# Encoder layer with expert-choice MoE on one core: splits, row loads, routing rounds, waves and norm sums in a new order, and idle turns at the head

## The reference

```python
h = rmsnorm(x, norm_mix)
u_b, u_c, u_x, u_f = split(h @ w_in)                  # 1024 -> 3*512 + 512
y_conv = rmsnorm(short_conv_mixer(u_b, u_c, u_x, conv_w), g_conv)
y_four = rmsnorm(real(fft2(u_f, axes=(seq, group of 64))), g_fourier)
x = x + concat(y_conv, y_four) @ w_out
h = rmsnorm(x, norm_ffn)
aff = softmax(h @ w_router)                           # 16 experts
gates, idx = top_k(aff.T, cap)                        # cap = 2*t//16 rows each
ye = (silu(xe @ w_gate) * (xe @ w_up)) @ w_down       # xe = h[idx], d_ff = 2816
x = x + scatter_add(ye * gates)
y = rmsnorm(x, norm_final)
```

## Time and profile before

| | |
|---|---|
| median of 3 runs | 2486.88 us (2484.79 to 2487.03) |
| the profiled execution | 2488.08 us, span 2486.2 us |
| mean granted clock of TensorE | 0.989 |
| PE busy | 2424.6 us (98%) |
| VectorE busy | 1611.8 us (65%) |
| ScalarE busy | 1358.4 us (55%) |
| GpSimd busy | 261.6 us (11%) |
| DMA | 628.13 MB, 253 GB/s |

### The profile page before, as it was taken

How to read it: one execution, slowest core, us unless ns; L and a number is a source line. 1 busy time by engine, 2 the same in 40 slices (tenths; PEclk the granted TensorE clock), 3 DMA queues, 4 the chain that set the end, 5 groups by cost and what they waited for, 6 DMA issues and landing times.

```text
span 2486.2 us, 45242 instructions
## 1 busy us (share of the span) xinstructions
PE 2424.6 (98%) x18368; PEld 1901.5 (76%) x18368; DVE 1611.8 (65%) x1331; ACT 1358.4 (55%) x1258; POOL 261.6 (11%) x234
## 2 busy tenths in 40 slices
PE   8999998699999999999999999999999999999996
PEld 7988887577777777777777777777777777777775
DVE  5443438766666666667666666666767676767665
ACT  6322343355555556565656565655555555555564
POOL 0020143102010202010201020102010101010102
PEclk9999999799999999999999999999999999999998
DMA  6002242568787878787878787878787878787877
GB/s 208 22 26 71 85 160 102 180 257 317 261 316 263 317 262 319 262 317 262 318 262 318 262 318 261 319 257 320 260 320 261 319 261 318 260 319 261 318 287 279
DMA packets 295966, 628.13 MB, mean 253 GB/s; under 512 B 21360, under 2 KB 72688, under 8 KB 295536
## 3 DMA queue, kind: packets, MB, share of 16 engines
q1 hardware_dynamic: 284160, 587.87, 64.2%
q0 software_dynamic: 11632, 37.51, 5.0%
HBM read 599.10 MB, written 26.21 MB: 252 GB/s over the span
## 4 chain that ended last, share of the span: by engine, by line
PE 92%; DVE 3%; issue 2%; DMA 1%; ACT 1%; POOL 0%; SPq 0%; POOLq 0%; DVEq 0%; ACTq 0%
PE ps L386 21%; PE ps L387 20%; PE ps L388 20%; PE ps L1618 12%; PE ps L1370 8%; PE ps L1626 6%; PE ps L1636 2%; DVE i L1135 1%; PE ps L1575 1%; DVE v L1133 1%; DVE A L1138 0%; PE ps L1390 0%; PE ps L1645 0%; DMA fx<-acc_dram 0%; DMA raw<-in_w_gate_dram 0%
## 5 line engine op out<-in xcount | busy, mean ns | idle before, releaser
L1249 DVE TENSOR_TENSOR spl_l<-raw,spl_h 128x2048 fp32r<-128x2048 f32 x528 | 1209.1, 2292 | 542.3 <-ACT spl_h L842 537.5
L842 ACT ACTIVATE spl_h<-raw 128x2048 fp32r<-128x2048 f32 x528 | 1011.8, 1917 | 583.6 <-PE ps L388 393.1
L386 PE MATMUL ps<-spl_h,xT 128*128 128x512 f32 x1408 | 554.1, 394 | 0.5 <-DVE xT L1254 0.4
L387 PE MATMUL ps<-spl_l,xT 128*128 128x512 f32 x1408 | 549.0, 390 | 0.0
L388 PE MATMUL ps<-spl_h,xT 128*128 128x512 f32 x1408 | 548.2, 389 | 0.0
L386 PEld LDWEIGHTS ps<-spl_h,xT 128*128 128x128 f32 x1408 | 264.2, 188 | 75.6 <-issue 19.1
L1618 PE MATMUL ps<-raw,xTs 128*32 128x256 f32 (+1 forms) x6144 | 314.2, 362 | 0.0
L388 PEld LDWEIGHTS ps<-spl_h,xT 128*128 128x128 f32 x1408 | 264.3, 188 | 56.1
L387 PEld LDWEIGHTS ps<-spl_l,xT 128*128 128x128 f32 x1408 | 264.3, 188 | 53.0
L386 PE MATMUL ps<-spl_h,g 128*128 128x512 f32 x704 | 279.1, 397 | 3.3 <-DVE spl_l L1249 3.3
L387 PE MATMUL ps<-spl_l,g 128*128 128x512 f32 x704 | 275.4, 391 | 0.0
(11 more groups left out here) (247 smaller groups left out, 1999.1 us busy)
## 6 DMA issues: line engine op xcount, KB each, us to landing
raw<-in_w_up_dram SPq DMA_DIRECT2D x352, 512.0 KB, 7.9
raw<-in_w_gate_dram SPq DMA_DIRECT2D x352, 512.0 KB, 9.3
raw<-in_w_down_dram SPq DMA_DIRECT2D x176, 1024.0 KB, 14.7
win_raw<-in_w_in_dram SPq DMA_DIRECT2D x16, 512.0 KB, 3.9
xt<-in_x_dram SPq DMA_DIRECT2D x10, 512.0 KB, 9.7
xr<-in_x_dram SPq DMA_DIRECT2D x10, 512.0 KB, 4.1
acc_dram<-xr SPq DMA_DIRECT2D x10, 512.0 KB, 2.7
xn_dram<-xn SPq DMA_DIRECT2D x10, 512.0 KB, 2.9
```

What stands on the lines that cost most here:

```text
L386: eng.matmul(o, a_h, b_h, start=first, stop=False, skip_group_check=True)
L387: eng.matmul(o, a_h, b_l, start=False, stop=False, skip_group_check=True)
L842: act.activation(spl_h[:, i % SPL, :], raw[:, slot_of(i), :], ACT.Copy).then_inc(sh_ok, 1)
L1249: dve.tensor_tensor(spl_l[:, i % SPL, :], raw[:, slot_of(i), :], spl_h[:, i % SPL, :].bitcast(F32), ALU.subtract).then_inc(sl_ok, 1)
```

## The change

It has seven parts. (1) At the head PE runs 24 transposes of the identity ahead of its first turns and 7 behind the first two. (2) In round 6 the waves stand behind steps 0, 2 and 4 instead of 0, 1 and 2. (3) The ten norm sums of tile 0 are split in 2, 4 and 4 and stand inside `half(..., 1, ...)`, and with them the wait for the last split of w_out (wol_ok) stands ahead of all of them. (4) In tiles 1, 2, 3, 5, 6, 7 and 9 the turn of the rows stands ahead of step 3 of the second half instead of ahead of the half. (5) VectorE's rounds 4 to 15 of half 0 move: rows 5 and 7 have one round less, none stands between the early rounds and the second sum, and three instead of one stand behind row 7. (6) Around the first gather the idle turns are 50 and 14 instead of 40 and 10. (7) In the last expert rows 3 to 5 move from unit INS+6 to behind the splits of unit INS+7's turn, and POOL issues the loads of rows 6 to 9 ahead of the stores of rows 3 to 5; FX is 7.

```diff
-FX = 6
-ROWS_STOP = {2: (0, 1, 2), 3: (3, 4, 5)}
-ROWS_UNIT = {INS + 8: (6, 7), INS + 9: (8, 9)}
+FX = 7
+ROWS_STOP = {2: (0, 1, 2)}
+ROWS_UNIT = {INS + 7: (3, 4, 5), INS + 8: (6, 7), INS + 9: (8, 9)}
...
-            for t in range(3, FX):
+            for t in range(3, FX - 1):
                 load_rows(t)
             for t in range(3):
                 store_rows(t)
...
-            for t in range(3, FX):
-                store_rows(t)
             pool.wait_ge(pe_s, (E - 1) * SAMPLE + NC + 1)
-            for t in range(FX, TILES):
+            for t in range(FX - 1, TILES):
                 load_rows(t)
-            for t in range(FX, TILES):
+            for t in range(3, TILES):
                 store_rows(t)
...
             rows(4, 0, None, None, None, None, (0, 0, 1))
-            rows(5, 1, (0, 1, 3), None, None, (0, 4, 1), (0, 5, 1))
-            rows(6, 0, (0, 6, 2), None, None, (0, 8, 1), (0, 9, 1))
-            rows(7, 1, (0, 10, 3), None, None, (0, 13, 1), (0, 14, 1))
-            top(0, 15, 1)
+            rows(5, 1, (0, 1, 3), None, None, None, (0, 4, 1))
+            rows(6, 0, (0, 5, 3), None, None, None, (0, 8, 1))
+            rows(7, 1, (0, 9, 3), None, None, None, (0, 12, 1))
+            top(0, 13, 3)
...
             pe.wait_ge(ident_ok, 4)
+            idle_turns(24)
             for t in range(2):
                 turn_x(t)
+            idle_turns(7)
...
-                    if 3 <= n < 3 + JH and k < 3:
-                        waves(n - 3, k)
+                    at = (0, 2, 4) if n == 2 + JH else (0, 1, 2)
+                    if 3 <= n < 3 + JH and k in at:
+                        waves(n - 3, at.index(k))
...
+                ends = [n for n in range(2) if t == GROUPS[n][1]]
                 if t == 0:
                     pe.wait_ge(qs_ok, JH - 1)
                     pe.wait_ge(rn_rt, 1)
-                    norm_sums(qc, 0)
                     pe.wait_ge(wol_ok, KD)
+                    between = {0: lambda: norm_sums(qc, 0, 0, 2), 1: lambda: norm_sums(qc, 0, 2, 6),
+                               2: lambda: norm_sums(qc, 0, 6, TILES)}
+                elif ends:
+                    rows_turned(t - 1)
+                    between = {1: lambda: router(ends[0]), 2: lambda: logits_turned(ends[0])}
                 else:
-                    rows_turned(t - 1)
+                    between = {3: lambda: rows_turned(t - 1)}
                 pe.wait_ge(ysl_ok, t * 2 + 2)
                 pe.wait_ge(x2_ok, t + 1)
-                ends = [n for n in range(2) if t == GROUPS[n][1]]
-                half(t, s, 1, of_done, {1: lambda: router(ends[0]), 2: lambda: logits_turned(ends[0])} if ends else {})
+                half(t, s, 1, of_done, between)
...
-            idle_turns(40)
+            idle_turns(50)
             gathered(1)
-            idle_turns(10)
+            idle_turns(14)
```

More of the change, by code:

```diff
@@ L1437, in waves, with norm_sums, idle_turns @@
                 last.then_inc(ds_done, 1)
-            def norm_sums(q, col):
-                for t in range(TILES):
+            def norm_sums(q, col, a=0, b=TILES):
+                for t in range(a, b):
                     last = pe.matmul(bank(7)[:, col + t:col + t + 1], q[:, t * P:(t + 1) * P], ones[:, 0:1],
                                      start=True, stop=True)
-                last.then_inc(nrm_ps, 1)
+                if b == TILES:
+                    last.then_inc(nrm_ps, 1)
+            def idle_turns(count):
+                for _ in range(count):
+                    pe.transpose(bank(0)[:, 0:P], ident[:, :], ident[:, :])
             pe.wait_ge(ident_ok, 4)
+            idle_turns(24)
             for t in range(2):
                 turn_x(t)
+            idle_turns(7)
             project_ahead(0, 0, 256, 2, {(0, 7): 2, (1, 7): 3})
@@ L1526, in rows @@
                     pe.wait_ge(rn_rt, 1)
-                    norm_sums(qc, 0)
                     pe.wait_ge(wol_ok, KD)
+                    between = {0: lambda: norm_sums(qc, 0, 0, 2), 1: lambda: norm_sums(qc, 0, 2, 6),
[3 more added lines that the diff above has]
+                    between = {1: lambda: router(ends[0]), 2: lambda: logits_turned(ends[0])}
                 else:
-                    rows_turned(t - 1)
+                    between = {3: lambda: rows_turned(t - 1)}
                 pe.wait_ge(ysl_ok, t * 2 + 2)
                 pe.wait_ge(x2_ok, t + 1)
-                ends = [n for n in range(2) if t == GROUPS[n][1]]
-                half(t, s, 1, of_done, {1: lambda: router(ends[0]), 2: lambda: logits_turned(ends[0])} if ends else {})
+                half(t, s, 1, of_done, between)
                 for n in ends:
                     group_turned(n)
-            def idle_turns(count):
-                for _ in range(count):
-                    pe.transpose(bank(0)[:, 0:P], ident[:, :], ident[:, :])
             def group_turned(n):
```

## The result

The changed kernel takes 2567.28 us (median of 4 runs, 2565.16 to 2570.07), beside 2486.84 of the kernel before on the same chip: ratio 1.0326, 95% interval 1.0308 to 1.0344. It is 80 us slower, where I had forecast 10 us faster.

A forecast was written before the change was run, and what follows sets the result against it. PE was taken to bound the kernel, with 92% of the chain. Terms -1.8 - 2.4 + 2.7 - 3.4 + 0.2 - 6.2 = -10.9 took 2488.08 to 2477.2 us; range 2475 to 2479.3, with rivals 1 to 3 2474.2 to 2480.5.

The forecast's parts named there:

- the one that ended slower (5): Output projection, tile 0: idling before the norm sums drops PE's clock and the sums keep it low; 2506 us, chance 0.01.
- Head, -1.8: Kernel start: 24 and 7 idle turns delay nothing and raise PE's clock for later work; -1.8 us, bounds 0 and -2.
- Rival 1: Head without gain: PE's clock is low again when tile 2 comes, since two waits stay; 2479.0 us, chance 0.15.
- Waves, -2.4: Last Fourier block: the new order removes PE's 0.92 us wait and the 1.5 us clock fall behind it; -2.4 us.
- Norm sums, +2.7: Output projection, tile 0: split sums stand on the path, tile 1 late; even chance of a clock fall; +2.7 us.
- Rounds, -3.4: Routing on VectorE: moved rounds and row turns remove PE's waits of 1.80 and 1.58 us; -3.4 us.
- Gather, +0.2: First gather: 50 and 14 idle turns end slightly later than the gathered rows need; +0.2 us, bounds 0 and +0.8.
- The end, -6.2: Last expert: earlier last split and loads of rows 6 to 9 bring the last scaling forward; -6.2 us, bounds -3.5 and -7.

The follow-up runs named there:

- no_turns: The changed kernel with its 45 added idle turns (24 and 7 at the head, 10 and 4 at the gather) taken out again; 2483.1 us, ratio 0.9975.
- tail_alone: The kernel before with only the change's part at the end (last expert's norms, last split, loads ahead of stores); 2479.9 us, ratio 0.9969.
- slot_128: The whole changed kernel with PE's expert loop made to begin at slot 128 of a 256-instruction fetch block; 2483.0 us, ratio 0.9976.
- slot_32: The whole changed kernel with PE's expert loop made to begin at slot 32 of a fetch block; 2555.6 us, ratio 1.0270.
- slot_192: The whole changed kernel with PE's expert loop made to begin at slot 192 of a fetch block; 2488.7 us, ratio 1.0002.
- sums_alone: The kernel before with only the norm sums dealt out over the second half, and the moved wait for wol_ok; 2495.6 us, ratio 1.0029.
- sums_back_128: The changed kernel with PE's loop at slot 128 and the norm sums in one piece ahead of the second half; 2476.9 us, ratio 0.9958.
- slot_64: The whole changed kernel with PE's expert loop made to begin at slot 64 of a fetch block; 2546.2 us, ratio 1.0235.
- shift_44: The kernel before with 88 waits (44 instructions, no matmuls) added on PE at the head; 2507.6 us, ratio 1.0080.
- sums_back_173: The changed kernel with the norm sums in one piece and PE's loop at slot 173; 2477.6 us, ratio 0.9962.

## Why the prediction was wrong

**The step that failed** is the second sentence of it: "The middle of the run, the experts from 476 us to about 2440 us, is PE work without holes, and the change leaves its loop alone, so I looked only where PE waits or runs slowly". (The first expert starts at 473.43 us, which changes nothing.) The change leaves the loop's code alone, but not its place: 45 turns, 90 instructions less one wait, went in ahead of it. The sum has no term for that, and no rival has it: the one that ended slower (5) rested on the clock. What stood in its place is 84.5 us, 13 borders at 6.5. Everything outside the loop came to -7.4 us in the profiled execution, against -10.9; without the gaps it would have taken 2565.2 - 84.5 = 2480.7 us, just above the range's end of 2480.5. What is missing of the -10.9 lies ahead of the output projection, where head and waves were to give 4.2 us: it starts at 297.87 us, before at 297.93.

**Head, -1.8:** -0.3 at the second weight slice, and -0.3 where the 512-wide products of the rounds start (45.47, before 45.78). Not even that is shown to be the turns' doing: no_turns and tail_alone, without turns at the head, get there at 44.53 and 44.46. Rival 1 was right in what it said: the clock is high during the turns and low again behind the two waits that stay. It was the likelier case, and had 0.15. That the turns would raise the clock was right, against the rule of the Trainium skill ("TensorE: Matmul & The Clock Gate", Part 4): 16 turns of x in 2.24 us and not 3.65.

**Waves, -2.4:** the wait and the fall behind it went, as laid out. In the changed kernel all but 0.1 came back before the output projection (297.87 us, before 297.93): 1.18 us of a wait for `win_l`, and 0.27 x 4 + 0.16 x 4 = 1.7 by the clock at 218 us. In slot_128 and no_turns, where the clock did not fall there, the same place came at 295.6 and 295.4. That looks like a gain of 2.3 to 2.5, but tail_alone, with the old head and the old waves, comes there at 295.10: it has the wait, and the clock stays up behind it.

```profile
156.02 0.30 PE L386 MATMUL ps<-tsm,Y_h 128*128 128x66 f32 x1 [0.92 <-DVE yfour L1011]
```
```profile
158.00:162.00 4.00, 4.00 (x22) 3.42 (x21) 0.58 (x4) 0.00 (x0) 3.33 (x2) 1.00 0.01 2
```

So the step that was wrong here is to have put the fall down to the wait for certain. Over all profiled executions the granted clock between 155 and 166 us is 0.84 in five of nine kernels with the old order of the waves, and 1.00 in all nine with the new; between 216 and 228 us it is 0.86 in four of the nine and three of the nine. One wait was exchanged for another, and what the new order seems to gain is that a fall comes less often. What the forecast lacked besides is the question what else lies beside the work that moves: the split of `win_l` came 3.0 us earlier and GpSimd's squares 2.0 us later, so that more of the split ran beside them (last section).

**Norm sums, +2.7:** the mechanism was right in every row: wait of 2.45 us ahead of the first sum, sums ended 311.05, tile 1 2.2 us late. The term was the mean of two cases, 2.0 without and 3.5 with a fall of the clock. The first came in the changed kernel, the second in no_turns, slot_32, slot_192 and sums_alone; there the fall was mis-sized, in no_turns 4.6 us on top (50.54 us from the start of the output projection to the third turn of rows in the changed kernel, 55.15 in no_turns), since it lasted from 303 to 317 us and not over eight matmuls. The 2.2 us are also no measure of what the split sums cost, for the profile before had a fall of its own behind its sums (0.91 from 300 to 320 us, 1.8 us). Where neither has one, the way from the start of the output projection to the first expert is 174.6 us with the sums split (slot_128) and 170.7 with them in one piece (sums_back_128): 3.9 us.

**Rounds, -3.4:** PE's waits for the normed row of tiles 5 and 7 are gone, and VectorE's second sum of tile 8 starts at 414.90, not 416.48, in spite of the 2.3 us by which it is all later from the norm sums: -3.9.

**Gather, +0.2:** as measured: the lists are 1.3 us earlier (460.48 and 461.80), the first expert 1.1.

**The end, -6.2:** -6.3 in the trace, in every row as laid out; -7.2 in tail_alone. Both the mechanism and the size were right.

## What to carry to other kernels

A loop whose instructions are fetched anew in every iteration has a place, and every instruction ahead of it on its engine moves it. Whoever adds work ahead of such a loop counts the instructions added (a matmul counts twice, by its weight load) and looks at the border of two iterations in the trace, even if the loop's code is the same; better still, the loop is pinned to a slot that measured well. In a measurement of small parts the loop is pinned first: 80 us of its placing hid the 5 us that the change gains at slot 128, and the 9 to 10 with the sums put back. And a part is judged against several executions, not by one profile before: a fall of the clock in that one profile was taken here for something that the change removes.

## What the runs showed of the hardware that was not expected

- The jump back to the head of a loop of 1498 instructions on PE, with a hint at its head, waits 4.7 us with the head at slot 0 of 256, 4.5 at 5, 3.8 at 32, 3.2 at 64, 0.6 at one of 13 borders at 128, nothing at 173 and 192. At 217 the wait is 1.0 us, 5.1 us behind the jump, where by the count of instructions the head's block ends. Why the head's block is asked for so late at the low slots, and why at 192 no packet comes ahead of the border, is open: no run looked inside the sequencer.
- The granted clock falls to 0.50 behind a gap of 4.4 us. Behind one of 3.2 it does at most borders of slot_64, but at 982.67 us it does not (1.00 from 983 to 987 us). Behind one of 1.2 it mostly does not: in shift_44 PE's matmuls go on 0.23 us apart behind the gap at 725, and only from 2361.8 to 2365 us, behind another of these gaps, is it 0.50.
- The same ten norm sums (20 records) at 217 to 219 us were followed by full clock in the kernel before and by 0.73 and 0.84 in the changed one, where they stand 1.6 us earlier. In sums_back_173 it did not fall there, in sums_back_128 it did. A fall of this kind can't be counted on, in either direction; it moves these kernels by 1.7 us, and at the norm sums of tile 0 by 4.6.
- VectorE's split of a weight slice, eight pieces and 2.19 us where GpSimd stands still (183.98 us), took far longer while GpSimd worked on `qf`:

```profile
L961 DVE SCALAR_TENSOR_TENSOR win_l<-win_raw,gmix,win_h 128x128 fp32r<-128x128 f32 x8 | 12.6, 1645 | 1.0 <-ACT win_h L665 1.0
```
```profile
177.58 2.94 POOL L523 TENSOR_TENSOR qf<-qf,sqf 128x1280 f32<-128x1280 f32 x1
```

It began at 168.84 and took 12.6 us, ending behind GpSimd's last operation at 180.52 (in the kernel before, 171.85 and 8.1 us, GpSimd's last ending at 178.5). The Trainium skill ("Trainium Architecture — The Big Picture", What this means for kernel authors) has VectorE and GpSimd share a pair of ports by "an exclusive lock (not a bandwidth split)"; these rows agree, but no run here took GpSimd's work away.
- Executions of one kernel without gaps differed by 7 to 10 us on one chip (slot_128: 2478.72 to 2485.58, slot_192: 2485.96 to 2496.45). The profiled run of slot_192 has eight short waits of PE, 7.5 us in all, for a split whose weights were loaded late. These, and the fall at its norm sums (granted clock 0.74 from 300 to 320 us, 1.00 in slot_128), are what separates slots 128 and 192, as far as the traces tell; whether the slot has a part in them is open.
